# One packed table word per expert for TensorE, the last h turned in the gate bank, and the final norm on two engines, in a two-block model with 32 experts

## The reference, cut to what matters

```python
g = xb @ w_gate[e] + b_gate[e]
u = xb @ w_up[e] + b_up[e]
g = jnp.minimum(g, SWIGLU_LIMIT)
u = jnp.clip(u, -SWIGLU_LIMIT, SWIGLU_LIMIT)
glu = g * jax.nn.sigmoid(SWIGLU_ALPHA * g)
return ((u + 1.0) * glu) @ w_down[e] + b_down[e]
```

## Time and profile before

| | |
|---|---|
| median of 3 runs | 1482.06 us (1481.13 to 1484.61) |
| profiled execution, its own time | 1486.34 us |
| its span, first to last instruction | 1484.2 us |
| PE busy | 1271.9 us, 86% of the span |
| weights and other data moved | 466.27 MB, mean 314 GB/s |
| mean granted TensorE clock | 0.947 of full speed |

### The profile page before, as it was taken

The page is one execution under the profiler, slowest core; times in us unless marked ns, Lnnn a source line. Parts: engine busy times, 40 slices in busy tenths (PEclk is TensorE's granted clock), DMA queues, the critical chain, the costliest instruction groups (busy, mean ns, idle before and its releaser), DMA issues.

```text
span 1484.2 us, 27736 instructions
## 1 busy us (share of the span) xinstructions
PE 1271.9 (86%) x10508; PEld 625.3 (42%) x10509; DVE 460.7 (31%) x1074; ACT 210.8 (14%) x500; POOL 44.3 (3%) x77
## 2 busy tenths in 40 slices
PE   7999999999999999999979886674667987886996
PEld 6757577664674433333323332221222332332342
DVE  1525434344576423222222221121112322231322
ACT  1212022111162111111111110010001101110201
POOL 0000000001010000000000000000000000000000
PEclk9999999999999799999999998788779998998999
DMA  9812173130830757999999999999999999999793
GB/s 351 308 57 86 58 280 117 57 130 31 293 114 7 302 227 331 376 405 430 428 430 427 429 429 427 429 430 427 429 429 427 429 427 428 430 427 429 314 431 151
DMA packets 61693, 466.27 MB, mean 314 GB/s; under 512 B 6496, under 2 KB 10332, under 8 KB 36956
## 3 DMA queue, kind: packets, MB, share of 16 engines
q1 hardware_dynamic: 58620, 462.63, 75.6%
q0 software_dynamic: 624, 2.10, 0.4%
q10 hardware_dynamic: 2416, 1.08, 0.3%
HBM read 464.74 MB, written 1.05 MB: 314 GB/s over the span
## 4 chain that ended last, share of the span: by engine, by line
PE 66%; DMA 28%; issue 3%; DVE 2%; ACT 0%; ACTq 0%; POOLq 0%; SPq 0%; DVEq 0%; POOL 0%
DMA ring<-in_w_up_dram 26%; PE bank L1237 18%; PE bank L817 11%; PE bank L824 8%; PE bank L1247 7%; PE bank L990 3%; PE bank L1263 3%; PE bank L1255 2%; PE bank L1218 2%; DMA ring<-in_w_down_dram 2%; PE bank L1156 1%; PE bank L1181 1%; PE bank L1040 1%; PE bank L1375 1%; PE bank L1339 1%
## 5 line engine op out<-in xcount | busy, mean ns | idle before, releaser
L1237 PE MATMUL bank<-ring,mem 128*32 128x512 f32 x2864 | 397.9, 664 | 160.0 <-DMA ring<-in_w_up_dram 108.6
L1237 PEld LDWEIGHTS bank<-ring,mem 128*32 128x32 f32 x2864 | 107.0, 120 | 396.9 <-issue 394.1
L817 PE MATMUL bank<-ring 128*128 128x256 f32 x768 | 168.5, 380 | 0.0
L1247 PE MATMUL bank<-ring,mem 128*32 128x256 f32 x2592 | 156.7, 382 | 2.8 <-DMA ring<-in_w_down_dram 2.3
L817 PEld LDWEIGHTS bank<-ring 128*128 128x128 f32 x768 | 145.2, 190 | 21.1 <-issue 1.7
L824 PE MATMUL bank<-ring 128*128 128x512 f32 (+2 forms) x320 | 123.9, 545 | 4.3 <-DVE ring L1472 4.3
L2116 DVE TENSOR_SCALAR mem<-bank 64x512 f32<-64x512 f32 x48 | 32.8, 683 | 275.1 <-PE bank L1237 275.1
L774 ACT ACTIVATE x_mem<-bank 128x256 f32 x49 | 18.8, 384 | 620.4 <-PE bank L1339 620.4
L1247 PEld LDWEIGHTS bank<-ring,mem 128*32 128x32 f32 x2592 | 76.1, 109 | 63.7 <-issue 18.9
L824 PEld LDWEIGHTS bank<-ring 128*128 128x128 f32 x320 | 61.5, 195 | 60.9 <-issue 52.7
L1263 PE MATMUL bank<-mem,cg 32*128 32x256 f32 x784 | 70.0, 426 | 9.4 <-DVE mem L2136 9.3
(11 more groups left out here) (355 smaller groups left out, 1051.2 us busy)
## 6 DMA issues: line engine op xcount, KB each, us to landing
ring<-in_w_gate_dram SPq DMA_DIRECT2D x64, 2048.0 KB, 31.0
ring<-in_w_up_dram SPq DMA_DIRECT2D x54, 2048.0 KB, 25.7
ring<-in_w_down_dram SPq DMA_DIRECT2D x53, 2048.0 KB, 26.3
ring<-in_w_in_dram SPq DMA_DIRECT2D x19, 2048.0 KB, 11.7
x_mem<-in_w_down_dram SPq DMA_DIRECT2D x11, 2048.0 KB, 24.9
x_mem<-in_w_up_dram SPq DMA_DIRECT2D x10, 2048.0 KB, 32.3
ring<-in_w_out_dram SPq DMA_DIRECT2D x6, 2048.0 KB, 8.1
ring<-in_w_in_dram SPq DMA_DIRECT2D x2, 1056.0 KB, 8.0
```

Of the source, the lines that this page charges most:

```text
L817: i = mm(b[:, S * j:S * j + S], w[:, k, P * (c + j):P * (c + j + 1)], hT[:, k, :], start=(k == 0), stop=(k == KC - 1))
L1237: i = mm(gate_up_bank(q), xT[:, at:at + T], w[q // 2][:, c, 512 * (q % 2):512 * (q % 2 + 1)], start=False, stop=(h == 1 and c == 3), skip_ ...
L1247: i = mm(YB[quarter[q], 0:QD], hT_sb[:, at:at + T], w[:, c, cols_of[q]], start=(h == 0 and c == 0), stop=(h == 1 and c == 3), skip_group_c ...
```

## The change

Three things are done.

First, DVE makes one more table, `packed`, with three more instructions between `n_through` and `hid_at`: for expert e it holds (blocks of e minus 1) times 512, plus (blocks of e-1 minus 1) times 64, plus the first block of e-1. `count_ready` now goes to 6 and everybody waits for 6. PE reads one word per expert and takes the three numbers out with shifts and masks in registers. Behind the last expert nothing is read: the numbers are carried over.

Second, the last block's h is turned into a part of the gate bank GB in place of YB. PE no longer waits there for DVE's copy of y but for its own last `biases`, which write to that bank (a new semaphore `bias`).

Third, the final norm. DVE first multiplies the four banks by the weights alone (banks 2 and 3, then 0 and 1, each after ACT has read its own pair), while ACT squares; then, once the power is there, ACT scales tokens 0 to 127 in SBUF and stores them from its own queue, and DVE scales tokens 128 to 255 and SP stores them in two halves.

```diff
+PACK_DOWNS, PACK_COUNT = 64, 512
...
+        LAST_HTB = GB[:, 0:QD]
...
-            sp.wait_ge(count_ready, 5)
+            sp.wait_ge(count_ready, 6)
...
-            for c in range(TC):
-                sp.wait_ge(x_ready, 2 * DEPTH + 7 + c)
-                sp.dma_start(out[0, P * c:P * (c + 1), :], xn[:, c, :]).then_inc(out_done, 16)
-            sp.wait_ge(out_done, 16 * TC)
+            for h in range(2):
+                part = slice(512 * h, 512 * (h + 1))
+                sp.wait_ge(xn_ready, 2 * DEPTH + 3 + h + 1)
+                sp.dma_start(out[0, P:2 * P, part], xn[:, 1, part]).then_inc(out_done, 16)
+            sp.wait_ge(out_done, 16 * 3)
...
-            turned_hidden(blocks)
+            turned_hidden(blocks, LAST_HTB)
             unread = ring[:, 0, 0:2 * D].rearrange("p (n d) -> p n d", n=4)
-            for c in range(TC):
-                act.wait_ge(ex["out"], 1)
-                for h in range(2):
-                    n = 2 * c + h
-                    i = A(unread[:, n, :], OUT[n][:, :], ACT.Square, scale=D ** -0.5, accum_out=small[:, 64 + n:65 + n])
-            i.then_inc(act_res, 1)
+            act.wait_ge(ex["out"], 1)
+            for n in range(4):
+                if n == 2:
+                    act.wait_ge(ex["weighted"], 2)
+                i = A(unread[:, n, :], OUT[n][:, :], ACT.Square, scale=D ** -0.5, accum_out=small[:, 64 + n:65 + n])
+                i.then_inc(act_res, 1)
+            act.wait_ge(ex["weighted"], 4)
+            act.wait_ge(pow_res, DEPTH * POW_L + 6)
+            for h in range(2):
+                part = slice(512 * h, 512 * (h + 1))
+                i = A(xn[:, 0, part], xn[:, 0, part], ACT.Copy, scale=small[:, 32:33])
+            i.then_inc(x_ready, 1)
+            act.wait_ge(x_ready, 2 * DEPTH + 7)
+            act.dma_start(out[0, 0:P, :], xn[:, 0, :]).then_inc(out_done, 16)
...
-                before_e = table(n_first, one(e - 1), 0, MAX_BLOCKS - 2)
-                downs = table(n_blocks, one(e - 1), 1, S // T)
-                count = table(n_blocks, one(e), 1, S // T)
+                of_e = table(packed, one(e), 0, PACK_COUNT * (S // T) - 1)
+                before_e = of_e & (PACK_DOWNS - 1)
+                downs = ((of_e >> 6) & (S // T - 1)) + 1
+                count = (of_e >> 9) + 1
...
-            last = table(n_first, static(E - 1), 0, MAX_BLOCKS - 2)
-            count = table(n_blocks, static(E - 1), 1, S // T)
-            blocks = table(n_total, slice(0, 1), E, MAX_BLOCKS - 1)
-            pe.wait_ge(ex["y_out"], last + 1)
+                last, count = gate_up_then_down(rounds * RING_EXPERTS + at + 1, static, at, rounds)
+            blocks = last + count
+            pe.wait_ge(ex["bias"], blocks + 1)
             pe.wait_ge(ex["xt_out"], blocks + 1)
             pe.wait_ge(ex["ht_out"], blocks + 1)
             pe.wait_ge(ex["h"], blocks + 1)
             pe.sem_inc(banks_clear, 1)
-            turn_hidden().then_inc(ex["ht"], 1)
+            turn_hidden(LAST_HTB).then_inc(ex["ht"], 1)
...
+            st.go(ts(packed_high[:, 1:E], nblk[:, 1:E], float(PACK_COUNT), -float(PACK_COUNT + PACK_DOWNS), ALU.mult, ALU.add))
+            st.do(stt(out=packed_low[:, 1:E], in0=nblk[:, 0:E - 1], scalar=float(PACK_DOWNS - 1), in1=ncum[:, 0:E - 1],
+                      op0=ALU.mult, op1=ALU.add))
+            tt(packed[:, 1:E], packed_high[:, 1:E], packed_low[:, 1:E], ALU.add).then_inc(count_ready, 1)
...
-            res.n += 1
+            v.wait_ge(roww_in, 48)
+            v.wait_ge(ex["out"], 1)
+            for n in (2, 3, 0, 1):
+                if n == 0:
+                    res.n += 2
+                    res.wait()
+                c, part = n // 2, slice(512 * (n % 2), 512 * (n % 2 + 1))
+                tt(xn[:, c, part], OUT[n][:, :], roww[:, part], ALU.mult).then_inc(ex["weighted"], 1)
+            res.n += 2
             res.wait()
             powered(stt(out=small[:, 0:2], in0=small[:, 64:68:2], scalar=NORM_EPS, in1=small[:, 65:69:2], op0=ALU.add,
                         op1=ALU.add))
-            v.wait_ge(roww_in, 48)
-            for c in range(TC):
-                for h in range(2):
-                    part = slice(512 * h, 512 * (h + 1))
-                    i = stt(out=xn[:, c, part], in0=OUT[2 * c + h][:, :], scalar=small[:, 32 + c:33 + c], in1=roww[:, part],
-                            op0=ALU.mult, op1=ALU.mult)
-                    i.then_inc(x_ready, 1) if h else i.then_inc(dve_step, 1)
+            v.wait_ge(ex["weighted"], 4)
+            for h in range(2):
+                part = slice(512 * h, 512 * (h + 1))
+                ts(xn[:, 1, part], xn[:, 1, part], small[:, 33:34], None, ALU.mult).then_inc(xn_ready, 1)
```

More of the change, by code:

```diff
@@ L249, in build @@
         n_blocks, n_first = sb("n_blocks", [P, E], I32), sb("n_first", [P, E], I32)
-        n_through = sb("n_through", [P, E], I32)
+        n_through, packed = sb("n_through", [P, E], I32), sb("packed", [P, E], I32)
         hid_at = sb("hid_at", [P, MAX_BLOCKS], I32)
@@ L263, in build @@
         negL, rsum = piece(TC), piece(TC)
-        nblk, ncum = piece(E), piece(E)
+        nblk, ncum, packed_high, packed_low = (piece(E) for _ in range(4))
         slot_at, slot_gate = piece(TC, TABLE), piece(TC, TABLE)
@@ L329, in build @@
               ("sel", "xs", "xs_out", "xt", "xt_out", "g", "uc", "gc", "eg", "h", "ht", "ht_out", "hs", "y", "y_out", "sum", "added",
-               "selg", "gt", "gt_out", "bsel", "out")}
+               "selg", "gt", "gt_out", "bsel", "bias", "out", "weighted")}
         class Steps:
@@ L549, in next_hidden @@
                 pool.tensor_copy(hT_sb, hT_all[:, bass.ds(at, QD)]).then_inc(ex["hs"], 1)
-            pool.wait_ge(count_ready, 5)
+            pool.wait_ge(count_ready, 6)
             blocks = pool.value_load(n_total[0:1, 0:1], min_val=E, max_val=MAX_BLOCKS - 1)
@@ L768, in _, with turned_hidden @@
             A(as_chunks(xs_sb), by_chunk(XGB[:, 0:QD]), ACT.Copy).then_inc(ex["xs_out"], 1)
-            act.wait_ge(count_ready, 5)
-            def turned_hidden(j):
+            act.wait_ge(count_ready, 6)
+            def turned_hidden(j, src=HTB):
                 at = act.value_load(hid_at[0:1, bass.ds(j, 1)], min_val=0, max_val=(HIDDEN - 1) * QD)
                 act.wait_ge(ex["ht"], j + 1)
-                A(hT_all[:, bass.ds(at, QD)], HTB, ACT.Copy).then_inc(ex["ht_out"], 1)
+                A(hT_all[:, bass.ds(at, QD)], src, ACT.Copy).then_inc(ex["ht_out"], 1)
             def gate_up(j):
@@ L1254, in biases @@
                     of = slice(E * (q // 2), E * (q // 2 + 1))
-                    mm(gate_up_bank(q), bsel[of, :], bias[of, 512 * (q % 2):512 * (q % 2 + 1)], start=True, stop=False,
-                       skip_group_check=True)
+                    i = mm(gate_up_bank(q), bsel[of, :], bias[of, 512 * (q % 2):512 * (q % 2 + 1)], start=True, stop=False,
+                           skip_group_check=True)
+                i.then_inc(ex["bias"], 1)
             def add_up(turn):
@@ L1328, in _ @@
             gather(XGB).then_inc(ex["xs"], 1)
-            pe.wait_ge(count_ready, 5)
+            pe.wait_ge(count_ready, 6)
             pe.wait_ge(bias_in, 32)
@@ L1334, in _, with turn_hidden @@
             biases()
-            def turn_hidden():
+            def turn_hidden(dst=HTB):
                 for c in range(4):
-                    i = tp(HTB[:, 2 * T * c:2 * T * (c + 1)], h_sb[:, P * c:P * (c + 1)], ident[0:2 * T, 0:2 * T])
+                    i = tp(dst[:, 2 * T * c:2 * T * (c + 1)], h_sb[:, P * c:P * (c + 1)], ident[0:2 * T, 0:2 * T])
                 return i
@@ L1396, in gate_up_then_down @@
                     down(first + count, before_e + b, weights)
+                return first, count
             static = lambda e: slice(e, e + 1)
@@ L2095, in _ @@
             v.wait_ge(tr_used, n_tr[0])
-            v.wait_ge(count_ready, 5)
+            v.wait_ge(count_ready, 6)
             v.sem_inc(ex["gt_out"], 1)
```

1 line of the change is left out of this document (removed).

## The result

The changed kernel took 1480.19 us (median of 20 runs, 1474.13 to 1484.51). The kernel before, run beside it 20 times, took 1487.2 us (1481.13 to 1493.38; the three runs shown ahead of the prediction are among them). The ratio is 0.995, with a 95% interval of 0.9934 to 0.9966: by that ratio faster by 7.4 us, between 5.1 and 9.8; the two medians lie 7.0 us apart. The prediction had taken 6.9 us off 1482.06 and so said 1475.2, in a range from 1471.5 to 1479.0. **The size of the change was right, the time was not:** 1480.19 lies 1.2 us above the range, since the three runs gave a level of before that was 5.1 us too low.

The account below looks back on a forecast made before the run. PE was taken to bound the expert stage to about 600 us, DMA to 1371 us, then PE again. Savings of 2.9 + 2.2 + 1.1 + 0.7 = 6.9 us off 1482.06 gave 1475.2, range 1471.5 to 1479.0.

Parts of the forecast that it names:

- The level: Profiled execution lay 4.3 us above the median of the runs shown; same difference taken from 1482.06, giving 1475.2.
- The sum of the change: Whole kernel: 2.9 + 2.2 + 1.1 + 0.7 = 6.9 us less.
- s = 1.1 us per gap: Between experts: packed word saves 1.4 us of sequencer time, less 0.3 for shifts and masks; 1.1 us (0.8 to 1.3).
- The low clock step: Rival, chance 0.18: 1.2 GHz step behind the longest gap between experts goes too, 1.7 us more; 8.6 us, 1473.5.
- Head 2.9 us: Ahead of 660 us: two gaps give 2.2 us, closing queue idle 0.7; loads come 2.9 us earlier (1.6 to 4.4).
- Fields worked out again in the loops: Rival, chance 0.05: shifts and masks redone at each wait in gate_up and down loops cost 15.3 us; 1490.5.
- The pause in the stream: Loads landing at 660.3 and 666.3: earlier issue closes 1.1 us beyond the 4.9 pace, 0.7 of it counted.
- End 2.2 + 1.1 us: Behind 1371.4 us: two table gaps give 2.2 us (1.6 to 2.6), earlier last down product 1.1 us (0.6 to 1.2).
- The turning: Behind the last expert: with words and wait gone, turning h follows at once, last down product starts 1.1 us earlier.
- Final norm 0.7 us: End of span: shared DMA engines limit the 1 MB store, so 0.7 us less (0 to 1.1), not 1.1 by issues.
- Three DVE instructions, the last load: Added table instructions, and the last load landing 10 us ahead of use: no cost; 0.6 us if cover were gone.
- The signs: Right: one read per expert, gap waits 0.3 to 0.9 us, last load wait near 1368.5, tail 8.3 us or less.

Follow-up runs that it names:

- e2: The kernel before with only the last h turned in the gate bank, three table words kept: 1485.16 us, ratio 0.9996.
- e3: The kernel before with the new final norm alone: 1488.11 us against 1485.15, ratio 0.9995.
- e5: The kernel before with three more table reads for each of experts 13 to 21, loop over turns cut in three: ratio 1.0013.
- e9: The changed kernel run again as it is, beside one with the fields held in registers: 1478.33 us, ratio 0.9942 to the kernel before.
- e1: The kernel before with the packed word alone, old turning and old final norm: 1481.55 us against 1485.15, ratio 0.9975.
- e7_stores: The changed kernel with fields held in registers and ACT storing each half as soon as it is scaled: 1476.49 us against 1485.97, ratio 0.9935.
- e6_ends: The kernel before with three more table reads for experts 1 to 3 and the last four, loop cut in three: ratio 1.0075.
- e8_head: The kernel before with one packed word for experts 1 to 3 alone, three words elsewhere, loop cut: 1482.11 us against 1485.59, ratio 0.9976.

## Why the prediction was right or wrong

**The level: wrong, and this is the step that failed.** "I take the same difference from the median" put the forecast on the 1482.06 us of three runs and gave that number no width. Of all 91 runs of before the median is 1485.55. They lie in four groups: 15 up to 1482.06, 43 from 1483.55 to 1487.52, 25 from 1488.77 to 1490.96, and 8 from 1493.19 to 1493.85. Two of the three runs that were shown are of the lowest group. The profiled execution's 1486.34 was nearer to the centre than the median I moved away to. From 1487.2, the level beside the changed kernel, the same sum gives 1480.3 against 1480.19. Most of what spreads the traces is visible in the table: the first expert starts at 510 us with 7 to 8.5 us of clock lost and at 516.5 with 15.4. The runs agree: the mean granted clock is 0.948 in the lowest group and 0.939 in the highest, in the 71 runs beside the experiments. A width for the level was to be had ahead of the prediction: its four executions already lay 5.2 us apart (1481.13 to 1486.34). The rule cited on the phase of the gate was a hint too, and I used it only for one step.

**The sum of the change: right, in part by luck.** 6.9 us, against 7.4 (5.1 to 9.8) by the runs and 6.3 by the pair of traces. Two things that the sum left out nearly cancel: the low clock step, 1.7 us more gained, and the fields worked out again in every block, some 2 us lost. Term by term:

- *s = 1.1 us per gap*: right. The six gaps of the two ends fell by 0.95 to 1.14 us. One load, one fused instruction and the assert are what is left.
- *The low clock step*: wrong in the main case, right as a rival. I kept it out because one execution can't show whether it belongs to the gap. Twelve traces do: five of five, none of seven. With it the head should have gained 4.6 us. The Trainium skill's statement on the phase ("TensorE: Matmul & The Clock Gate", "Part 1: The HAM clock gate") fits the steps ahead of the experts, where clock lost goes from 6.8 to 15.4 us in the same instructions, and the fourth gap, where one execution of six has a step; behind the first gap no trace bears it out. That steps differ between executions is shown; that the phase is the reason is not.
- *Head 2.9 us*: the number held (3.2 in the pair, 2.3 between the means of before, e2, e3, e5 and of after, e9, e1), for reasons that cancel. The clock step gave 1.7 us more. Working the fields out again took 1.1 us back. With registers the same means differ by 4.6 us, which looks like 2.9 + 1.7, but 0.9 of it is the step that runs on past the first expert. Without that part the gain is 2.6 us with the fields worked out again and 3.7 with registers, so 2.0 of the 2.9 us came beside the clock step. Also, the upper bound of 4.4 us does not follow from its words: 2 x 1.3 and half of 2.6 are 3.9.
- *Fields worked out again in the loops*: I gave this as the way to be slower, with 0.9 us per block and a break-even of 0.4. The mechanism is there and its size is not: 0.4 us of sequencer time per block, most of it under PE's running matmuls, and 0.14 to 0.28 us that show ahead of second and later products. It took off some 2 us, too little to turn the sign.
- *The pause in the stream*: partly right. The two landings of the earlier trace rows were to be 4.9 us apart instead of 6.0. After, the load issued at 641.2 lands behind 19.7 us, at 660.9, and the next behind 10.2, at 666.1, so 5.2 apart. The last line of each issue's rows, after:

```profile
DMA to landing us min/median/max: 19.7/19.7/19.7
...
DMA to landing us min/median/max: 10.2/10.2/10.2
```

  But PE reaches the point of that issue 5 us earlier relative to the first expert and the landing comes only 3.2 us earlier. The load ahead of it lands 2.4 us earlier, and this one can follow it by the pace of 4.9 us at best in place of 5.9, so no more than 3.4 of the 5 us could arrive. The 2.4 go back to a load issued at 616.5 (3.4 us earlier than its like of before, relative to the first expert), which takes 10.2 us where its like took 9.3. It takes 8.2 to 10.5 us in the traces; why is open, and no run was made on it.
- *End 2.2 + 1.1 us*: 2.4 came in the pair, 3.0 to 3.3 in the kernels with registers. So both terms were sized right, and the 0.9 us missing are the fields again. The turning gave its 1.1 us only with both parts, as the text's two reasons for the 1.11 us (words and wait) had it.
- *Final norm 0.7 us*: 0.62 to 0.64 in every trace with that order of stores. The last issue is 5.17 us behind the last matmul, against 6.3 before, 1.1 earlier, as said, and the first is 0.7 earlier; the end gained the smaller number. The output's transfer, after, as it ends (columns as in the earlier trace rows):

```profile
1476.40:1477.60 1.20, 0.00 (x0) 0.00 (x0) 0.40 (x2) 0.92 (x2) 0.00 (x0) 0.50 0.26 96
1477.60:1479.10 1.50, 0.00 (x0) 0.00 (x0) 0.00 (x0) 0.00 (x0) 0.00 (x0) 0.50 1.05 401
1479.10:1480.90 1.80, 0.00 (x0) 0.00 (x0) 0.00 (x0) 0.00 (x0) 0.00 (x0) 0.50 0.48 184
```

  The share is 1.05 for 1.5 us, where the earlier trace rows have 0.99. The Trainium skill has it in "DMA: Bandwidth & Descriptors", "Issuing engines are not separate DMA queues", that transfers issued by several engines share the same 16 DMA engines and that a second issuer saves only sequencer time. e7_stores agrees: last issue 0.6 us later, end 0.06 us later.
- *Three DVE instructions, the last load*: nothing of either shows. The stream between the cuts is 705.1 us against 705.2, and no wait for a load stands behind the one at 1371.1.
- *The signs*: the one read, the last `down` 1.65 us behind the matmuls before it and the earlier last store came. The gap of 1.02 us at the first expert is above the 0.9 named. PE's last wait for a load ends at 1371.1 and not near 1368.5, since the first expert starts 3.0 us later. The tail is 8.70 us and not 8.3 or less, a bound that was tighter than the sum's own term (9.3 - 0.7 = 8.6).

## What to carry to other kernels

Before a difference is taken from a median of a few runs, ask how far single executions of that kernel lie apart and put that into the range: here three runs missed the level by 5.1 us, where the range left 3.8 us above the forecast. A value unpacked from a table word is cheap only if it is unpacked once; look in the sequencer's records for register operations at lines inside the loops, and move it into a register ahead of them. Where two things end at the same wait, price them together, since either alone gives little: here 0.1 to 0.2 us of 1.1.

## What the runs showed that was not expected

- A pause of PE of 2.1 us or more behind the first expert was followed by a step to 1.2 GHz in all five traces that have it, so the price of this gap was 1.7 us above its length (3.4 in e6_ends, where the gap is 3.63 us). One-word gaps, shorter by a microsecond, had none there. Gap length alone does not decide it: at the fourth gap one of six of 1.9 to 2.0 us was followed by a step, and one gap of 3.05 us by none.
- The same program starts its first expert between 510.2 and 516.5 us (after, two executions), with 8.5 and 15.4 us of clock lost ahead of it.
- Issuing a transfer held ACT's sequencer for 0.42 us (e7_stores), and the second half of the scaling started that much later.
- e5_mid shows two more pauses of about 1.3 us each in the load stream, at loads 79 and 147, and e8_head one of 1.0 us at load 42. The kernels whose loop is in one piece have none between load 32 and load 180; what made them is open.
